# Projection, gate and expert weights stored by the host as the tiles that the loads read, in a one-core encoder-layer kernel

## The reference, cut to what matters

```python
h = modulate(rmsnorm(x, norm1_g[l]), sh1, sc1)
z = h @ w_in[l]                       # w_in: 1024 x 2048
...
ga, gb, gc = jnp.split(jax.nn.sigmoid(h @ gate_w[l] + gate_b[l]), N_BRANCHES, axis=-1)   # gate_w: 1024 x 3072
mixed = ga * (ya @ proj_a[l]) + gb * (yb @ proj_b[l]) + gc * (yc @ proj_c[l])
x = x + g1[:, None, :] * (mixed @ w_out[l])
...
# 2048 tokens, each sent to the top 2 of 32 experts, in blocks of 128 slots of one expert
return (jax.nn.silu(xblk @ w1[e]) * (xblk @ w3[e])) @ w2[e]   # w1, w3: 32 x 1024 x 512; w2: 32 x 512 x 1024
```

## Time and profile before

| | us |
|---|---|
| the three executions | 2948.14, 2960.63, 2951.82 |
| their median | 2951.82 |
| the profiled execution's own time | 2954.11 |
| its span, first to last instruction | 2952.2 |

### The profile page before, as it was taken

How to read it: one execution, slowest core, us unless ns; L and a number is a source line. 1 busy time by engine, 2 the same in 40 slices (tenths; PEclk the granted TensorE clock), 3 DMA queues, 4 the chain that set the end, 5 groups by cost and what they waited for, 6 DMA issues and landing times. The chain is left out here.

```text
span 2952.2 us, 41275 instructions
## 1 busy us (share of the span) xinstructions
PE 2782.0 (94%) x13642; PEld 2215.4 (75%) x13643; DVE 1905.2 (65%) x3149; ACT 1469.0 (50%) x2361; POOL 369.0 (13%) x287
## 2 busy tenths in 40 slices
PE   6999998999999988999998999987999999999996
PEld 5768886787877776788876878875777777777774
DVE  6754774746464655644455773457888888888884
ACT  4414664656565553233244342124666666666662
POOL 2101220000000001101010001110222222222211
PEclk8999999999999998999999999998999999999998
DMA  6475324040403137211148995428989989777884
GB/s 234 143 248 193 105 103 164 23 155 31 154 30 129 44 125 237 68 47 50 51 168 295 352 343 204 168 93 301 337 280 298 374 299 304 239 226 228 283 258 134
DMA packets 287584, 554.82 MB, mean 188 GB/s; under 512 B 28748, under 2 KB 95564, under 8 KB 285144
## 3 DMA queue, kind: packets, MB, share of 16 engines
q1 hardware_dynamic: 269048, 492.06, 46.7%
q0 software_dynamic: 14400, 52.44, 7.2%
q10 hardware_dynamic: 4000, 8.53, 0.9%
HBM read 418.21 MB, written 143.15 MB: 190 GB/s over the span
## 5 line engine op out<-in xcount | busy, mean ns | idle before, releaser
L2715 DVE TENSOR_TENSOR moe_w_lo<-moe_W,moe_w_hi 128x1024 fp32r<-128x1024 f32 x384 | 460.4, 1219 | 85.6 <-ACT moe_w_hi L2643 71.7
L2643 ACT CAST moe_w_hi<-moe_W 128x1024 fp32r (+1 forms) x384 | 402.0, 1052 | 148.1 <-PE moe_h1b L2566 76.2
L1631 PE MATMUL project_bank<-h_lo,w_hi 128*128 128x512 f32 x512 | 201.0, 393 | 0.0
L336 PE MATMUL att_bank<-h_hi,w_hi 128*128 128x512 f32 x384 | 168.9, 440 | 13.0 <-ACT att_gates L418 8.1
L2591 PE MATMUL moe_yb<-moe_W,moe_hT 128*128 x384 | 172.5, 592 | 0.0
L427 ACT ACTIVATE att_S<-att_S,att_nm,q_scale 128x128 f32<-128x128 f32 (+15 forms) x128 | 165.7, 1296 | 4.4 <-DVE att_nm L530 4.0
L2564 PE MATMUL moe_h1b<-moe_w_hi,moe_xT_hi 128*128 128x512 f32 x384 | 155.9, 406 | 4.8 <-DVE moe_xT_lo L2726 4.8
L521 DVE TENSOR_SCALAR_CACHE_REDUCE att_S<-att_bank 128x512 f32<-128x512 f32 x192 | 122.3, 687 | 54.8 <-PE att_bank L303 54.8
L338 PE MATMUL att_bank<-h_hi,w_lo 128*128 128x512 f32 x384 | 151.4, 394 | 0.0
L337 PE MATMUL att_bank<-h_lo,w_hi 128*128 128x512 f32 x384 | 151.2, 394 | 0.0
L2566 PE MATMUL moe_h1b<-moe_w_hi,moe_xT_lo 128*128 128x512 f32 x384 | 151.1, 393 | 0.0
(11 more groups left out here) (498 smaller groups left out, 6866.8 us busy)
## 6 DMA issues: line engine op xcount, KB each, us to landing
moe_W<-in_moe_w SPq DMA_DIRECT2D x96, 2048.0 KB, 13.8
w_raw<-in_gate_w SPq DMA_DIRECT2D x48, 512.0 KB, 3.8
out_sg<-gateT SPq DMA_DIRECT2D x32, 768.0 KB, 6.9
gateT<-att_gates SPq DMA_DIRECT2D x48, 256.0 KB, 2.0
gateT<-gate_out SPq DMA_DIRECT2D x48, 256.0 KB, 2.0
early<-in_ada_w SPq DMA_DIRECT2D x8, 1024.0 KB, 12.7
project_spare<-in_x SPq DMA_DIRECT2D x16, 512.0 KB, 6.9
zT<-project_oz SPq DMA_DIRECT2D x32, 256.0 KB, 3.5
```

The source lines that it names most:

```text
L336: pe.matmul(bank[7][:], w_hi[b][:, k, :], h_hi[:, k, at], start=k == 0, stop=False)
L1631: pe.matmul(bank[n % 4][:], w_hi[b][:, k, :], low[:, k, at512(tb)], start=False, stop=False)
L2643: nc.scalar.copy(w_hi[:, slot(p, first), :], raw(at, p)).then_inc(q["w13_high"], 1)
L2715: nc.vector.tensor_tensor(w_lo[:, own, :], raw(at, p), w_hi[:, own, :].bitcast(F32), ALU.subtract).then_inc(q["w1_low" if p < 4 else "w3_l ...
```

## The change

The host stores five inputs in another order before the launch. `w_in` and `gate_w` become a row of tiles of 128 x 8 x 128: group by group, and within a group partition by partition, so that what one partition gets is 4 KB in one stretch. `moe_w1` and `moe_w3` become, for each expert, 128 partitions of 8 x 512 elements (16 KB in one stretch), `moe_w2` 128 partitions of 4 x 1024 elements (16 KB). The loads read the same elements into the same tiles, in the same order and behind the same waits. No other instruction changes.

```diff
-    gate_w = g["gate_w"][0].rearrange("(k p) n -> p k n", p=P)
...
                 def load_w(c):
-                    at = c % (HEADS * CH) * P
-                    sp.dma_start(raw[:], gate_w[:, :, at:at + P]).then_inc(q["raw_ready"], 16)
+                    sp.dma_start(raw[:], g["gate_w"][c % (HEADS * CH)]).then_inc(q["raw_ready"], 16)
...
     def load(self, sp, j):
-        src = self.g["gate_w"][0].rearrange("(k p) n -> p k n", p=P)
-        sp.dma_start(self.tiles["raw"][:], src[:, :, bass.ds((self.c0 + j) * P, P)]).then_inc(self.raw_ready, 16)
+        sp.dma_start(self.tiles["raw"][:], self.g["gate_w"][self.c0 + j]).then_inc(self.raw_ready, 16)
...
-    w_in = g["w_in"][0].rearrange("(k p) n -> p k n", p=P)
-    gate_w = g["gate_w"][0].rearrange("(k p) n -> p k n", p=P)
...
                 def load_w(c):
-                    src = w_in[:, :, chunks[c][1] * P:(chunks[c][1] + 1) * P] if c < NC else gate_w[:, :, (c - NC) * P:(c - NC + 1) * P]
+                    src = g["w_in"][chunks[c][1]] if c < NC else g["gate_w"][c - NC]
...
-    w1, w3 = (g[n][0].rearrange("e (k p) n -> e p k n", p=P) for n in ("moe_w1", "moe_w3"))
-    w2 = g["moe_w2"][0].rearrange("e (k p) n -> e p k n", p=P)
+    w1, w3, w2 = (g[n] for n in ("moe_w1", "moe_w3", "moe_w2"))
...
+def laid(np, name, a):
+
+    if name in ("w_in", "gate_w"):
+        a = a[0].reshape(KD, P, -1, P).transpose(2, 1, 0, 3)
+    if name in ("moe_w1", "moe_w3", "moe_w2"):
+        a = a[0].reshape(NE, -1, P, a.shape[-1]).transpose(0, 2, 1, 3)
+    return np.ascontiguousarray(a)
...
-        a = _np.ascontiguousarray(inputs[name])
+        a = laid(_np, name, inputs[name])
```

## The result

The changed kernel takes 2963.38 us (median of 14 executions, 2958.49 to 2967.18); the kernel before, run beside it, 2953.73 (14 executions, 2947.82 to 2960.63). The ratio is 1.0032, 95% interval 1.0024 to 1.0041: 9.65 us slower by the medians, inside the 0.5% that the prediction called "same", but outside its range, whose upper end was 2963.0. The profiled execution of the changed kernel took 2958.49 us, with a span of 2956.6; that is its quickest, 4.4 us of span above the profiled one of before.

What follows compares the result with a forecast made beforehand. TensorE's instructions were taken to bound the kernel. Pooling -0.5 and tail -0.5 us, all else 0, sum to -1.0 us: 2953.1 us from the profiled 2954.11, or 2950.8 against the median of three, 2951.82; range 2942.0 to 2963 us.

Steps and rivals of the forecast that it cites:

- same: Whole kernel: a time within about 0.5% (14.8 us) of before, which a measurement can't tell from no change; chance 0.90.
- What bounds the kernel: Whole kernel: TensorE's instructions bound it; it was busy 800.00 of 800.00 us while the experts' weights stream in.
- Front: First two `w_in` loads: taken as 0, with bounds of a 0.9 us gain and 0.
- Pooling: ScalarE's 8.96 us wait for a `gate_w` load: load 0.45 us earlier, so -0.5 us; bounds 0 and -1.6.
- the price of short runs: All changed loads: 309 GB/s with 512-byte runs against 420 with mostly 8 KB runs, taken from rows, against the skill.
- Tail: Behind the experts' loop: its last add lands earlier, -0.5 us; at most 3.1 us gained or 4.4 us later.
- Experts' loop: Experts' weight loads: -0.35 us a load, but 0 on the path, as TensorE is busy throughout.
- long packets hold up GpSimd's transfers: Rival, experts' stage: 16 KB packets on SP's queue make GpSimd's gathers and adds land later, so slower; chance 0.06.
- The range: Whole kernel: 2942.0 us with all gaps closed, up to 2963 with the tail's loss, scatter and late gathers.
- D: Experts' stage: how much later a GpSimd gather or add lands beside 16 KB packets; between 2.3 and 4.4 us.
- TensorE waits only from D = 5.0: Experts' loop: the add's spare 1.0 us goes first; TensorE waits only once each landing is 5.0 us later.
- The rival's price: Experts' loop, saturated stretches: 11 blocks, 22 us for each microsecond of D beyond 5; 2974 us at D = 6.0.

Runs made afterwards that it cites:

- experts_rows: The changed kernel with the experts' weights back in row-major form (runs of 2 and 4 KB), `w_in` and `gate_w` tiles kept; 2952.12 us, ratio 0.9995 to the kernel before.
- first_copy_sp: gather_first with the copy of `acc` to `out` in rows of 4 KB, issued by SP in ScalarE's place; 2950.60 us, ratio 0.9994.
- runs_8k: The changed kernel with the experts' weights in two runs of 8 KB for each partition instead of one of 16 KB; 2953.53 us, ratio 1.0002.
- gather_first: The changed kernel, 16 KB runs kept, with GpSimd issuing the gather for four blocks on before it waits for the add to land; 2953.27 us, ratio 1.0000.
- experts_padded: The changed kernel with 64 bytes left free behind every k of the experts' weights, so runs end after 2 and 4 KB; 2954.43 us, ratio 1.0010.
- rows_copy_4k: experts_rows with ScalarE's copy of `acc` to `out` in rows of 4 KB instead of 64 KB packets; 2952.14 us, ratio 1.0001.

## Why the prediction was wrong

- **What bounds the kernel**: right. TensorE's instructions did, and the DMA's freed time bought nothing: the share fell by 0.05 and no block became shorter. That a transfer in this stretch is hidden "however slow it is" was too strong. It held for the weight loads; it didn't for GpSimd's, which had some 5.5 us to spare.
- **Front**: right as 0. SP's issue at the second `w_in` load fell from 12.77 to 2.06 us, ScalarE's wait from 3.78 to 3.16, and VectorE's wait that covers both stayed, 7.08 us after 7.09.
- **Pooling**: the load was 0.49 us quicker, 9.94 instead of 10.43 us from SP's issue to ScalarE's copy (1118.64 to 1128.58; before, 1118.87 to 1129.30). ScalarE's wait fell from 8.96 to 7.73 us and TensorE's gap from 1.64 to 1.06, the -0.5 us of the sum. A packet of 512 bytes had taken 27 ns of an engine at the median, one of 4 KB takes 159, which over 16 engines is 303 and 412 GB/s: it was right to go by the rows for the price of short runs. `experts_rows`, which holds front, project, attention and pooling alone, gives -0.05% with an interval of 0.25%: that agrees, and can't confirm half a microsecond.
- **Tail**: -0.5 us was forecast; the long block went from 27.70 to 26.44. In the twelve profiles that block runs from 26.4 to 29.0 us (but for `first_copy_sp`), so no single execution can say more.
- **Experts' loop**: here it failed. The rival "long packets hold up GpSimd's transfers" is what happened, and it had a chance of 0.06. That the time still is within 0.5% isn't to the forecast's credit: it is small because only eight blocks were hit.
- **The range**: its high end doesn't add up its terms. The tail's 4.4 us above 2951.8 and the runs' scatter of 8.8 give 2965.0 together, which would have held the measured 2963.4, and the kernel before itself came out at 2953.73 in 14 executions, 1.9 above the median of three that the range started from. Either would have made the range right without the mechanism.

The size of D was nearly right. The prediction bounded D, the delay of one landing, by 2.3 and 4.4 us. In the crowded blocks the gather's packets took 3.6 to 4.7 us longer than before, the add's 3.3 to 4.4 (table above: 5.7 - 2.1 to 6.8 - 2.1, and 6.9 - 3.6 to 8.0 - 3.6). **The step that failed is the condition: "TensorE waits only from D = 5.0".** It followed one gather behind one late add that had itself been issued in time. Nor had that add 1.0 us to spare in the crowded stretch: before, the one issued at 2325.49 landed at 2334.84, and the next copy of indices, which comes 0.54 behind a landing when it waits for one, stood at 2335.38. And the lateness is handed on: in the changed kernel the copies of indices at 2282.81, 2302.41, 2323.66 and 2345.14 come 4.5, 5.7, 8.0 and 8.0 us behind the start of TensorE's transposing, where 1.2 is usual. Once the gather is late enough, the next add is issued 2 us behind it and queues up behind its packets; that add's landing lets the next gather go; and so on, until GpSimd's cycle is a chain of its own: the gather to its last packet, then the add's packets and landing, then the next copy of indices. With the values of before this chain is 7.2 us for the gather (some 5.1 to its first packet and 2.1 for all of them), 3.6 for the packets of an add that stand right behind it, about 1 from the last of them to the copy of indices, and 1.1 from that copy to the next issue: 12.9 us, in a period of 18.40. (The 12.9 us of the expectations is another number: how much later both landings came, each from its issue.) The spare is 5.5 us for both delays together, so 2.75 for each and not 5.0, and that lies inside the bounds of D, 2.3 and 4.4: over most of its own range for D the prediction should have had TensorE waiting.

With the measured delays the chain gives 12.9 + 3.6 + 3.3 = 19.8 to 12.9 + 4.7 + 4.4 = 22.0 us, and the crowded blocks took 20.21, 20.38 and 21.49. For `runs_8k` the delays come to 1.7 + 1.6 = 3.3 us at most, below 5.5: GpSimd waits, TensorE doesn't. For `gather_first` the delays are there and the cycle no longer runs through both landings. All three agree with the chain; that the spare is 5.5 is bounded by the runs only between the 3.3 that cost nothing and the 6.9 that did.

The rival's price was off as well, in the other direction: it put 11 blocks under it and 22 us on each microsecond. Only eight blocks were longer, by 1.2 us in the mean. As a block gets longer the same loads fill less of it (the DMA share of 2360 to 2400 us is 0.90, where it was 1.04); that this is what holds the loss down is argued, and no run tests it.

That an engine alternates between queues by whole packets is what the page "DMA: Bandwidth & Descriptors" of the Trainium skill says in "Queues, rings and completion order". The trace agrees, a packet there being one contiguous run: 256 of 4 KB beside 274 of 16 KB. The same page, in "SWDGE vs HWDGE vs iDMA", gives a packet as preferably at most 4096 bytes and calls it the boundary at which the DMA engine switches; I didn't weigh that line, and it could have spoken against this change. The runs agree as far as they go: 2 and 4 KB cost nothing that can be measured here (but for the 0.1% of `experts_padded`, which is open), 8 KB delayed without cost, 16 KB cost 0.3%.

## What to carry to other kernels

Longer runs freed DMA time here and bought nothing, as TensorE waited for no load. Where another queue has small transfers with a deadline, the length of the neighbour's packets is part of their latency: check both together against the spare time, and count in series what one in-order engine issues in series, over several rounds of the loop and not one. And if a landing must be waited for, issue first what doesn't depend on it: that order made the kernel indifferent to runs of 16 KB.

## What the runs showed of the hardware that I had not expected

- A gain in the DMA engines' time and a loss in latency came together: the share fell from 0.87 to 0.82 while the longest landing of an add rose from 10.5 to 17.9 us.
- The run length of a copy from memory to memory (8 MB, beside one gather) hardly changed its duration, in one execution each: from ScalarE's issue to GpSimd's first read of `out` it was 31.1 us with packets of 64 KB (`experts_rows`, 2869.44 to 2900.56) and 30.8 with packets of 4 KB (`rows_copy_4k`, 2867.65 to 2898.45). What it changed was the issue, 2.53 and 5.99 us for four transfers on ScalarE's queue, and the neighbour's landing, 25.7 and 10.1 us.
- One access pattern of contiguous runs became one packet for each run here, up to 64 KB: none was split at a smaller size.
